# Two recurrent layers with the second token tile in mirror order, and their weights' low parts made by VectorE instead of GpSimd

## What is computed

```python
def _hgrn2(q_raw, f_raw, i_in, g_raw, lower_bound, out_norm):
    q = jax.nn.silu(q_raw.astype(F32))
    f = lb + (1.0 - lb) * jax.nn.sigmoid(z)
    log_f = jnp.log(jnp.maximum(f, F_FLOOR))
    k = (1.0 - lb) * jax.nn.sigmoid(-z)
    ...
    b = jnp.cumsum(lfb, axis=2)
    decay = jnp.where(tri, jnp.exp(jnp.where(tri, diff, 0.0)), 0.0)
    attn = jnp.einsum('bhtd,bhsd,bhtsd->bhts', qb, kb, decay)
    o = jnp.einsum('bhts,bhsv->bhtv', attn, vb) + jnp.einsum('bhtd,bhdv->bhtv', qb * jnp.exp(b), state)
```

## Time and profile before

| what | value |
|---|---|
| median of 3 runs | 1897.99 us (1897.94 to 1900.1) |
| the profiled execution, own time | 1899.83 us |
| its span, first to last instruction | 1897.9 us |
| mean granted TensorE clock | 0.999 |
| busy: PE, DVE, ACT, POOL | 1875.3, 1523.3, 1240.1, 403.3 us |
| first recurrent layer (hf to the output gemm) | about 461 to 603 us |
| second recurrent layer | about 788 to 930 us |

### The profile page before, as it was taken

How to read it: one execution, slowest core, us unless ns; L and a number is a source line. 1 busy time by engine, 2 the same in 40 slices (tenths; PEclk the granted TensorE clock), 3 DMA queues, 4 the chain that set the end, 5 groups by cost and what they waited for, 6 DMA issues and landing times.

```text
span 1897.9 us, 26327 instructions
## 1 busy us (share of the span) xinstructions
PE 1875.3 (99%) x9450; PEld 1578.4 (83%) x9450; DVE 1523.3 (80%) x1649; ACT 1240.1 (65%) x1484; POOL 403.3 (21%) x206
## 2 busy tenths in 40 slices
PE   9999999999999999999999999999999999999997
PEld 6888888888898888878888888888888888888886
DVE  6745367777576887697699999999999999999997
ACT  6654444444644444464488888888888888888876
POOL 6856870001824000282450000000000000000000
PEclk9999999999999999999999999999999999999999
DMA  9534556665434676534599999999999999999994
GB/s 284 170 119 134 178 186 218 224 221 172 142 122 133 206 242 221 163 120 134 176 383 395 391 380 376 386 397 368 389 365 388 396 365 388 366 387 396 370 395 188
DMA packets 251397, 523.68 MB, mean 276 GB/s; under 512 B 9944, under 2 KB 58720, under 8 KB 251184
## 3 DMA queue, kind: packets, MB, share of 16 engines
q1 hardware_dynamic: 243408, 504.00, 74.2%
q10 hardware_dynamic: 5680, 11.61, 1.7%
q0 software_dynamic: 2224, 6.95, 1.1%
HBM read 507.19 MB, written 15.34 MB: 275 GB/s over the span
## 4 chain that ended last, share of the span: by engine, by line
PE 93%; DVE 3%; POOL 1%; ACT 1%; issue 1%; DMA 0%; SPq 0%; DVEq 0%; ACTq 0%
PE bank L726 25%; PE bank L728 24%; PE bank L727 24%; PE bank L1081 6%; PE bank L1084 3%; PE bank L1160 2%; POOL w_lo_sb L655 1%; PE bank L849 1%; PE bank L1345 1%; PE bank L822 1%; PE bank L828 1%; DMA arena<-in_w_in 0%; PE bank L990 0%; PE bank L967 0%; DVE arena L2050 0%
## 5 line engine op out<-in xcount | busy, mean ns | idle before, releaser
L1971 DVE TENSOR_TENSOR w_lo_sb<-arena,w_hi_sb 128x1024 fp32r<-128x1024 f32 x672 | 807.8, 1223 | 73.8 <-ACT w_hi_sb L1499 43.6
L1499 ACT ACTIVATE w_hi_sb<-arena 128x1024 fp32r<-128x1024 f32 x672 | 711.2, 1062 | 168.7 <-PE bank L728 168.0
L726 PE MATMUL bank<-w_hi_sb,left_sb 128*128 128x512 f32 (+1 forms) x1400 | 553.4, 395 | 2.8 <-POOL w_lo_sb L655 2.8
L728 PE MATMUL bank<-w_hi_sb,left_sb 128*128 128x512 f32 (+1 forms) x1400 | 542.3, 387 | 0.0
L727 PE MATMUL bank<-w_lo_sb,left_sb 128*128 128x512 f32 (+1 forms) x1400 | 541.5, 387 | 0.0
L1519 ACT ACTIVATE w_hi_sb<-arena 128x1024 fp32r<-128x1024 f32 (+1 forms) x269 | 278.2, 1052 | 299.8 <-PE bank L728 220.8
L655 POOL TENSOR_TENSOR w_lo_sb<-arena,w_hi_sb 128x1024 fp32r<-128x1024 f32 (+1 forms) x134 | 341.6, 2569 | 552.0 <-ACT w_hi_sb L1519 551.2
L726 PEld LDWEIGHTS bank<-w_hi_sb,left_sb 128*128 128x128 f32 x1400 | 263.1, 188 | 61.1 <-POOL w_lo_sb L655 7.6
L728 PEld LDWEIGHTS bank<-w_hi_sb,left_sb 128*128 128x128 f32 x1400 | 262.9, 188 | 54.9
L727 PEld LDWEIGHTS bank<-w_lo_sb,left_sb 128*128 128x128 f32 x1400 | 263.4, 188 | 50.9 <-issue 0.7
L726 PE MATMUL bank<-w_hi_sb,hid_hi_sb 128*128 128x512 f32 x656 | 257.3, 392 | 0.1
(11 more groups left out here) (356 smaller groups left out, 1687.5 us busy)
## 6 DMA issues: line engine op xcount, KB each, us to landing
arena<-in_moe_w_gate SPq DMA_DIRECT2D x112, 1024.0 KB, 7.9
arena<-in_moe_w_up SPq DMA_DIRECT2D x112, 1024.0 KB, 8.0
arena<-in_moe_w_down SPq DMA_DIRECT2D x112, 1024.0 KB, 7.7
arena<-in_w_in SPq DMA_DIRECT2D x45, 1024.0 KB, 5.1
arena<-in_w_ffn_in SPq DMA_DIRECT2D x22, 1024.0 KB, 5.1
arena<-in_w_out SPq DMA_DIRECT2D x12, 1024.0 KB, 5.1
arena<-in_w_ffn_out SPq DMA_DIRECT2D x11, 1024.0 KB, 4.8
arena<-in_dense_w_gate SPq DMA_DIRECT2D x11, 1024.0 KB, 5.4
```

Of the source, the lines that this page charges most:

```text
L726: pe.matmul(out, still[0], moving[0], start=start, stop=False)
L728: return pe.matmul(out, still[1], moving[0], start=False, stop=stop)
L1499: act.activation(expert_buffer(w_hi_sb, j), expert_piece(j % MOE_SUBS), ACT.Copy) \
L1971: dve.tensor_tensor(expert_buffer(w_lo_sb, j), expert_piece(j % MOE_SUBS), expert_buffer(w_hi_sb, j).bitcast(F32), ALU.subtract) \
```

## The change

Three things, in both recurrent layers. (1) The second token tile is turned with a flipped identity where x enters and where the mixed output leaves, so that its 128 tokens lie in reverse order in between. In it the second half of a level's block then holds the keys. The key halves of tile 0 and of tile 1 fill one 512-word operand, the query halves another, and levels 1 to 7 take 4 matmuls and one bank; two masks (the new one is the transpose) pick each tile's block from it. Gate sums of the second tile use the other triangle, the causal table is mirrored. (2) What is laid out by token row must be mirrored too: the mean square of x's second tile and the second column of positions go through TensorE against the flipped identity (`mirror_column`, three times in all) and come back by a bank. (3) The low parts of all pieces from hf to hi are made by VectorE, in calls of `lo_to` written into its order; GpSimd keeps those of the output gemm. ScalarE makes two high parts ahead of the root in both layers.

```diff
-        by_vector = j < FIRST_SUBS or any(lo + BUFFERS <= j < hi + AFTER_FFN for lo, hi in ffn_range.values())
+        by_vector = j < FIRST_SUBS or any(lo + BUFFERS <= j < hi for lo, hi in ffn_range.values()) \
+            or any(span[f"hf_{l}"][0] <= j < span[f"hi_{l}"][1] for l in range(2))
...
-        level = [(f"hlev{n}_{layer}", T) for n in range(len(LEVELS) + 1)]
+        level = [(f"hlev{n}_{layer}", 1 if n else T) for n in range(len(LEVELS) + 1)]
...
+            def mirror_column(name, column, ready, number):
+
+                pe.wait_ge(sem(ready), number)
+                pe.matmul(pair(name, 0)[:, 0:1], flip, column, start=True, stop=True).then_inc(sem("pair_full"), 1)
...
-            gemm("gb0")
+            gemm("gb0", between={1: lambda: mirror_column("posT", pos_f[:, 1:2], "pos_ready", 1)})
...
-                gemm(f"hf_{l}", f"hT_l{l}", between={0: lambda: turn_x(f"l{l}", range(2, 4))})
+                gemm(f"hf_{l}", f"hT_l{l}", between={
+                    0: lambda: turn_x(f"l{l}", range(2, 4)),
+                    2: lambda: mirror_column(f"msT_{l}", ms_rows[:, 1:2], "ms_rows_ready", l + 1)})
...
-                    for t in range(T):
+                    for t in range(1 if n else T):
                         b = pair(f"hlev{n}_{l}", t)
                         for i in range(HG_HEADS):
                             at = (t * HG_HEADS + i) * P
-                            key, query = (n_X[n % 2], n_X[n % 2]) if n else (n_kT, n_qT)
+                            key, query = (n_X[n % 2][:, 0:512], n_X[n % 2][:, 512:1024]) if n else (n_kT, n_qT)
...
+            act.wait_ge(sem("merged"), 2)
+            act.dma_start(mirror_masks, A["mirror_masks"]).then_inc(sem("mirror_masks_landed"), 16)
...
+                split_to(span[f"hf_{l}"][1] + 2)
                 factor(f"l{l}")
                 if l == 0:
-                    split_to(span["hf_0"][1] + 2)
...
-                mean(ms, ms, D, "ms_ready")
+                if tag not in ("l0", "l1"):
+                    mean(ms, ms, D, "ms_ready")
+                    return
+                mean(ms_rows, ms, D, "ms_rows_ready")
+                lo_to(span[f"hq_{tag[1]}"][0] + 2)
+                copy_out(f"msT_{tag[1]}", 0, ms[:, 1:2], width=1)
+                dve.tensor_copy(ms[:, 0:1], ms_rows[:, 0:1]).then_inc(sem("ms_ready"), 1)
+                dve.wait_ge(sem("ms_ready"), told("ms_ready"))
...
+                lo_of("hf", 4)
                 mean_square(f"l{l}")
                 factor(f"l{l}")
...
                 absolute(tiles(n_tmp[0]), n_z, "z_abs")
+                lo_of("hq", 4)
                 soft = tiles(n_tmp[1])
                 if l == 0:
+                    lo_of("hg", 1)
                     dve.wait_ge(sem("z_soft"), 1)
...
                     mul(share, share, over(bound_rest, 1, T))
+                    lo_of("hg", 1)
                     dve.wait_ge(sem("z_soft"), 2)
...
                     dve.tensor_tensor(n_k, n_k, over(log_rest, 1, T), ALU.subtract).then_inc(sem("n_k_ready"), 1)
+                lo_of("hg", 4)
+                lo_of("c0", 1)
...
                 level_diff(1)
+                lo_of("c0", 3)
...
                 level_diff(2)
+                lo_of("c0", 4)
...
                 level_scale(2)
+                lo_of("c1", 2)
+                lo_of("hi", 1)
                 level_take(1)
                 level_diff(4)
+                lo_of("hi", 2)
                 level_scale(3)
                 level_take(2)
+                lo_of("hi", 3)
                 normalize_c()
+                lo_of("hi", 4)
                 rotate(lambda t: n_c[:, t, Q_RANK + KV_RANK:].rearrange("p (h d) -> p h d", h=1), 1)
                 level_take(3)
```

More of the change, by code:

```diff
@@ L89, in constants @@
     query = [r + P * t for t in range(T)]
+    mirrored = [np.arange(P), TOKENS - 1 - np.arange(P)]
+    mirrored_key = np.concatenate(mirrored)[None, :]
     half = HD // 2
@@ L96, in constants @@
     parts = {
-        "le": r <= c, "ge": r >= c, "gt": r > c, "lt": r < c, "ident": r == c, "ones": np.ones((P, P)),
+        "le": r <= c, "ge": r >= c, "gt": r > c, "lt": r < c, "ident": r == c, "flip": r + c == P - 1, "ones": np.ones((P, P)),
         "window": np.concatenate([np.where(abs(q - key) <= WINDOW, 0.0, MASKED) for q in query], 1),
-        "causal": np.concatenate([np.where(key <= q, 0.0, MASKED) for q in query], 1),
+        "causal": np.concatenate([np.where(mirrored_key <= q[:, None], 0.0, MASKED) for q in mirrored], 1),
         "iota": np.broadcast_to(np.arange(CAP), (P, CAP)),
@@ L107, in constants @@
         masks.append((r // (2 * h) == c // (2 * h)) & (r % (2 * h) < h) & (c % (2 * h) >= h))
-    return np.ascontiguousarray(table), np.ascontiguousarray(np.concatenate(masks, 1).astype(np.int32))
+    mirror_masks = [mask.T for mask in masks[1:]]
+    return [np.ascontiguousarray(table)] + [np.ascontiguousarray(np.concatenate(m, 1).astype(np.int32))
+                                            for m in (masks, mirror_masks)]
 def counter():
@@ L349, in over, with grid @@
             return ap.to_broadcast(shape)
-        le, ge, gt, lt, ident, ones = (const(c) for c in ("le", "ge", "gt", "lt", "ident", "ones"))
+        def grid(a, at, *dims):
+            return bass.AP(a.tensor, a.offset + at, [list(a.ap[0]), *[list(d) for d in dims]])
+        le, ge, gt, lt, ident, ones, flip = (const(c) for c in ("le", "ge", "gt", "lt", "ident", "ones", "flip"))
+        mirror = (ident, flip)
         window, causal = tiles(const("window")), tiles(const("causal"))
@@ L837, in pair, with transpose_all @@
                 return pair_bank[j % 4]
-            def transpose_all(name, source, k_tiles, first=0, ready={}, banks=None):
+            def transpose_all(name, source, k_tiles, first=0, ready={}, banks=None, order=(ident, ident)):
                 for i in banks or range(-(-k_tiles // 2)):
@@ L1250, in turn_mix @@
                     transpose_all(f"mixT_{l}", lambda k, t: (mix, n_o)[k // 4][:, t, (k % 4) * P:(k % 4 + 1) * P], KD,
[L1251 removed]
+                                  ready={2: (f"hg_mixed_{l}", T)}, banks=banks, order=mirror)
                 for t in range(T):
@@ L2339, in _, with lo_of @@
             for l in range(2):
+                def lo_of(name, pieces):
+                    lo_to(span[f"{name}_{l}"][0] + pieces)
+                lo_of("hf", 4)
                 mean_square(f"l{l}")
@@ L2401, in level_scale @@
                     dve.wait_ge(sem(f"level_exp_{l}"), 2 * n)
[L2402 to L2403 removed]
+                    X_query = halves(n_X[n % 2][:, 512:1024], half)
+                    part = X_query.rearrange("p n s c -> p s n c")
+                    dve.tensor_tensor(part, part, queries_of(n_qT, half), ALU.mult).then_inc(sem(f"level_ready_{l}"), 1)
+                    dve.wait_ge(sem(f"level_ready_{l}"), told(f"level_ready_{l}"))
                 def level_take(n):
[L2406 to L2414 removed]
+                    if n == 0:
+                        for t in range(T):
+                            b = tiles(bank_of(f"hlev0_{l}", t)[:, :], 4)
+                            mul(tiles(n_at[:, t * 512:(t + 1) * 512], 4), b, over(ident, 1, 4), "pair_read")
+                        return
+                    if n == 1 and l == 0:
+                        dve.wait_ge(sem("mirror_masks_landed"), 16)
+                    b = tiles(bank_of(f"hlev{n}_{l}", 0)[:, :], 4)
+                    masks = (level_masks[:, n * P:(n + 1) * P], mirror_masks[:, (n - 1) * P:n * P])
+                    for t in range(T):
+                        ins = dve.copy_predicated(tiles(n_at[:, t * 512:(t + 1) * 512], 4), over(masks[t], 1, 4), b)
+                    ins.then_inc(sem("pair_read"), 1)
+                    dve.wait_ge(sem("pair_read"), told("pair_read"))
                 def rotate(part, heads):
@@ L2695 @@
     nc = _bacc.Bacc("TRN2", target_bir_lowering=False, num_devices=1)
-    table, masks = constants()
+    table, masks, mirror_masks = constants()
     arrays, A = {}, {}
-    for name, value in {**inputs, "const_table": table, "level_masks": masks}.items():
+    for name, value in {**inputs, "const_table": table, "level_masks": masks, "mirror_masks": mirror_masks}.items():
         a = np.ascontiguousarray(value)
```

54 lines of the change are left out of this document (26 added, 28 removed).

## The result

| | before | after |
|---|---|---|
| median, us | 1898.22 (8 runs, 1897.94 to 1900.1) | 1904.13 (8 runs, 1902.67 to 1905.8) |
| ratio, 95% interval | | 1.0029 (1.002 to 1.0038) |
| profiled execution: own time / span | 1899.83 / 1897.9 | 1902.67 / 1900.1 |
| granted clock over the span | 0.999 in the profiled execution | 0.994 to 0.998 in the 8 runs |

By the ratio, the change makes the kernel 5.5 us slower; the forecast was 1897.7, no change. The profiled execution is the fastest of the changed kernel's eight, so its trace shows the loss at its smallest: 2.2 us of span.

The account below looks back on a forecast made before the run. TensorE, busy 99% of the span, was taken as the bound. Layer one -0.9, layer two +0.3 and the reflection of positions +0.3 summed to -0.3 us: forecast 1897.7 us, range 1889.5 to 1901.5.

Parts of the forecast that it names:

- Matmuls taken away: Levels 1 to 7 of both recurrent layers: half of each level's matmuls goes, 6.15 us per layer, 12.3 in all.
- A: Before hf's third piece: its low part comes late from VectorE, stalling TensorE 2.1 us in layer one, 1.7 in two.
- B: First layer, up to hg's third piece: later low parts just in time, +0.7 us net.
- C: Second layer, up to hg's third piece: hg's second low part late, a 4.0 us stall, +1.9 us net.
- D: Head projections: TensorE waits some 2.5 us; they start 0.6 us later in the first layer, 1.8 in the second.
- Rival 3: Clock falls in the second layer's stall before hg's second piece: 2 to 4 us lost, 1900 to 1902 us; chance 0.10.
- Step E: From the projections to the softmax, levels 4 to 7: -1.5 us per layer, bounds -0.9 and -3.6.
- Rival 1: Before the projections VectorE's chain ends in time, and the stretch to the softmax gives all: 1888.6 us; chance 0.22.
- Rival 2: No low part is late anywhere; only the matmuls and old waits count: 1880 us; chance 0.05.
- Rival 4: VectorE's operations stay long without GpSimd, so the second layer's gate chain takes some 9 us more: 1910; chance 0.03.

Follow-up runs that it names:

- filled_and_held: Changed kernel with its five long waits filled with idle matmuls and GpSimd held ahead of the output product's low parts: 1898.35 us, ratio 0.9993 to the kernel before.
- mended_part_earlier: Changed kernel, GpSimd making hf's third, fourth and hi's last two low parts, held before the output product's; VectorE making hg's second ahead of n_k: 1890.7 us.
- late_parts_early: Changed kernel, GpSimd making low parts of hf's third, fourth and hi's last two pieces, VectorE hg's second before its logarithm wait: 1893.01 us, ratio 0.9968.
- hg_part_early: Changed kernel with hg's second low part made ahead of VectorE's wait for the logarithm in the second layer: 1902.36 us, ratio 1.002 to the kernel before.
- mirror_alone: Changed kernel with GpSimd making the recurrent layers' low parts again, as before the change: 1895.05 us, ratio 0.9981 to the kernel before.

## Why the prediction was wrong

**Matmuls taken away: right.** L1179 has 144 instances (was 256), L666 94, L2002 175.

**Steps A to D, the places and lengths of the waits: right.** A: 1.95 and 1.49 us (2.1 and 1.7 forecast), restart at 469.68 (469.8). B: the low parts of the first layer's later pieces are in time, and the gate sums start at 492.00, 0.66 us later than before, where 0.7 was forecast. C: hg's second piece starts at 819.74 (820.0), with the gate operations at 1.22 us each. D: projections at 536.81 and 868.81, waits of 1.97 and 1.94 (2.5); 0.1 and 2.5 us later than before, where 0.6 and 1.8 were forecast. The second has the clock's 1.4 us in it, and so has hg's third piece, at 827.14 instead of the 826.3 forecast; without it both would lie 0.6 to 0.7 us earlier than forecast. A written order could be walked through here with durations of the old trace to within 0.7 us.

**Rival 3, the clock: the step that failed.** The forecast's sum has no term for the clock. The rival had a chance of 0.10, a price of 2 to 4 us, and one place. The argument "the stall only just gets there" took the one idle stretch that the old trace shows, some 4 us, for the least that matters; but a row that shows a fall after 4 us says nothing of 2. Counted over the profiled executions of the five kernels with unfilled waits: behind the wait of 3.6 us the clock fell in 3 of 3, behind waits of 1.9 to 2.0 in 3 of 13, behind those of about 1.5 in 0 of 6; each fall cost 1.4 to 1.7 us (4.29 to 4.44 us for a piece of 2.8 to 2.9, and 4.54 us for the projections' twelve matmuls of 2.86). With five such waits in the changed kernel, filling them gave 4.0 us in the median. The single profiled execution has one fall of 1.4 us; only the list of clocks of all runs, 0.994 to 0.998, tells that the others have more. An estimate: the fall at 820 takes 0.28 + 1.00 + 0.42 = 1.7 us of full clock (the windows from 818 to 824), 0.0009 of the span's mean; the eight runs' mean is 0.9960, that of the filled kernel's eleven 0.9983, which is two to three falls per run and, at 1.4 to 1.7 us each, the 4 us that the filling gave. The rates counted above would give 1.7 falls, so the profiled executions show too few (the changed kernel's is its fastest run); in which waits the others fell isn't shown. The Trainium skill (TensorE: Matmul & The Clock Gate, "Why this matters for your kernels") warns of idle gaps between bursts; by that rule this rival would rather happen than not. The trace agrees behind the wait of 3.57 us, at 0.50 from 820 to 822. The falls to 0.50 near 538 and 470 stand behind waits of 1.94 to 1.97 us, shorter than the gaps that it warns of; there the measurement decides.

**Step E: mis-sized.** -1.5 us per layer was forecast, -0.13 and -0.49 came. The step moved VectorE's work up with the projections but left GpSimd where it was. In fact GpSimd's low parts for the output product moved up by 1.66 us too (557.16 from 558.82), and ahead of an operation that had led them by 0.08 us; in the second layer they lead it likewise, 889.16 against 889.60. Held back, the stretch lost 1.2 us per layer (38.65 and 38.64 in `filled_and_held`), -1.3 and -1.7 against before: the forecast's size. The prediction knew the price (0.69 to 2.47 us beside GpSimd is the rule that it used in C) and did not ask who else would start earlier. The Trainium skill's rule (SBUF — State Buffer, "Who interferes with whom"), that a VectorE instruction with two SBUF inputs contends with a GpSimd one that reads SBUF, covers it. The trace agrees: 2.47 us behind GpSimd's start, 0.69 ahead of it.

**The sum.** By ratios: 1.0029 with everything, 1.0005 with the clock held (4.6 us), 0.9993 with GpSimd held as well (2.3 us). The second difference is no larger than the noise of one such pair, but all four pairs with and without the hold show it (3.2, 2.5, 2.3 and 2.7 us), beside the 1.2 us per layer of the traces. What is left, -1.3 us, with an interval of -3.0 to +0.4, holds the forecast's -0.3.

**Rivals 1, 2 and 4: did not happen.** The wait before the projections stood there, the parts were late, the operations short.

## What to carry to other kernels

A wait of 2 us on TensorE cost its length here and a draw for the clock (3 falls in 13); price both, per wait, and fill a wait that can't be removed with idle matmuls of no more than its length (worth 4.0 us here). When an engine takes over work, ask for each piece whether that engine has time at that place of its order: here 32 of 40 pieces fitted, and the other 8, with one piece that only had to stand ahead of a wait, turned +5.5 us into -8.8 (with GpSimd's hold). When a stretch moves up, every engine moves up, also the one that then gets in the way.

## What the runs showed that was not expected

The clock fell already behind waits of 1.94 to 1.97 us, in one execution and not in the next. Behind four waits of 1.7 to 1.9 us in other traces it stayed at 1.00: 1.73 at 819.33 in the kernel before, 1.86 in `mended_part_earlier`, 1.72 and 1.83 near 46 us in `late_parts_early` and `filled_and_held`. The spread of a kernel's runs does not tell it: 5.4 us with three such waits in `hg_part_early`, but 4.1 us in `mirror_alone` with none. The mean granted clock does: 0.998 to 0.999 in every run of the kernels whose waits stay under 1.9 us or are filled, down to 0.994 in those with a longer one left. Why a wait of one length sometimes keeps the clock was not tried. And a fall's price hardly depends on the wait: 1.4 to 1.6 us behind 3.57, 1.6 and 1.7 us behind 1.97 and 1.94.
